# Moving five small steps of a hybrid-mixer kernel from GpSimd to VectorE

## The reference, cut to what matters

```python
for l in range(DEPTH):                                  # DEPTH = 2
    x = x + 0.5 * g1 * swiglu(modulate(rms_norm(x)), w1, w3, w2)
    x = x + g2 * hybrid_mixer(modulate(rms_norm(x)))
    x = x + 0.5 * g3 * swiglu(modulate(rms_norm(x)), w1, w3, w2)

def hybrid_mixer(h):
    q, k, v, qi, ki, wi, u = split(h @ w_in)
    q, k, qi, ki = rope(q), rope(k), rope(qi), rope(ki)  # partial rotary
    attn = dsa_attention(q, k, v, qi, ki, wi)   # indexer scores, top 128 keys per query, softmax
    y = gelu(s5_ssm(u))                         # state-space scan
    y = y * sigmoid(y @ glu_w + glu_b)
    return concat(rms_norm(attn), rms_norm(y)) @ w_out
```

## Time and profile before

| | us |
|---|---|
| median of 3 executions | 2107.84 |
| lowest, highest | 2107.36, 2109.96 |
| the profiled execution | 2107.84 |
| its span, first to last instruction | 2106.0 |
| PE busy | 2033.2 (97%) |
| DVE busy | 1317.8 (63%) |
| ACT busy | 694.5 (33%) |
| POOL busy | 261.0 (12%) |

### The profile page before, as it was taken

The page is one execution under the profiler, slowest core; times in us unless marked ns, Lnnn a source line. Parts: engine busy times, 40 slices in busy tenths (PEclk is TensorE's granted clock), DMA queues, the critical chain, the costliest instruction groups (busy, mean ns, idle before and its releaser), DMA issues.

```text
span 2106.0 us, 25359 instructions
## 1 busy us (share of the span) xinstructions
PE 2033.2 (97%) x9588; PEld 1639.6 (78%) x9588; DVE 1317.8 (63%) x2052; ACT 694.5 (33%) x1061; POOL 261.0 (12%) x231
## 2 busy tenths in 40 slices
PE   6999899999799999999999999999998999999998
PEld 5788778877577788888888877788775778888886
DVE  6778846566875654543466697375779656545334
ACT  4332222341444422222343322233334534213223
POOL 0006900400100000000000195040001000000000
PEclk8999999999799999999999999999997999999999
DMA  8465556342102354533337455544420125453332
GB/s 290 122 212 186 157 156 184 89 113 81 56 21 59 102 180 140 178 93 100 91 118 224 139 171 155 162 145 109 105 69 21 41 86 175 120 189 116 106 93 78
DMA packets 395985, 264.77 MB, mean 126 GB/s; under 512 B 56560, under 2 KB 371672, under 8 KB 395864
## 3 DMA queue, kind: packets, MB, share of 16 engines
q1 hardware_dynamic: 387360, 260.94, 40.9%
q10 hardware_dynamic: 8504, 2.22, 0.6%
HBM read 254.98 MB, written 6.29 MB: 124 GB/s over the span
## 4 chain that ended last, share of the span: by engine, by line
PE 63%; issue 22%; DVE 9%; ACT 4%; DMA 1%; ACTq 0%; SPq 0%; POOL 0%; DVEq 0%; POOLq 0%
PE ps L1700 18%; PE ps L1701 17%; PE ps L1702 17%; DVE w_lo L1002 2%; DVE mod_acc L1023 2%; PE ps L1980 2%; ACT w_hi L697 1%; PE ps L1999 1%; PE ps L1924 1%; PE ps L2007 1%; PE ps L1990 1%; PE ps L2072 1%; DVE x L1108 1%; DMA stage<-in_ffn_w 1%; PE ps L2077 1%
## 5 line engine op out<-in xcount | busy, mean ns | idle before, releaser
L1700 PE MATMUL ps<-h_hi,w_hi 128*128 128x512 f32 x1728 | 686.3, 397 | 15.6 <-DVE w_lo L1002 12.9
L1701 PE MATMUL ps<-h_lo,w_hi 128*128 128x512 f32 x1728 | 677.6, 392 | 0.0
L1702 PE MATMUL ps<-h_hi,w_lo 128*128 128x512 f32 x1728 | 677.2, 392 | 0.0
L1002 DVE TENSOR_TENSOR w_lo<-stage,w_hi 128x1024 fp32r<-128x1024 f32 (+2 forms) x322 | 394.3, 1247 | 117.3 <-ACT w_hi L697 113.5
L1700 PEld LDWEIGHTS ps<-h_hi,w_hi 128*128 128x128 f32 x1728 | 326.7, 189 | 95.9 <-issue 14.6
L1702 PEld LDWEIGHTS ps<-h_hi,w_lo 128*128 128x128 f32 x1728 | 327.1, 189 | 69.8
L1701 PEld LDWEIGHTS ps<-h_lo,w_hi 128*128 128x128 f32 x1728 | 327.2, 189 | 65.6 <-issue 0.5
L697 ACT ACTIVATE w_hi<-stage 128x1024 fp32r<-128x1024 f32 (+2 forms) x322 | 318.9, 1016 | 173.4 <-PE ps L1702 165.1
L1700 PE MATMUL ps<-g_hi,w_hi 128*128 128x512 f32 x704 | 276.7, 393 | 0.8 <-DVE g_lo L1317 0.8
L1701 PE MATMUL ps<-g_lo,w_hi 128*128 128x512 f32 x704 | 274.2, 389 | 0.0
L1702 PE MATMUL ps<-g_hi,w_lo 128*128 128x512 f32 x704 | 274.2, 389 | 0.0
(11 more groups left out here) (302 smaller groups left out, 1839.8 us busy)
## 6 DMA issues: line engine op xcount, KB each, us to landing
stage<-in_ffn_w SPq DMA_DIRECT2D x210, 512.0 KB, 4.4
mod_stage<-in_mod_w SPq DMA_DIRECT2D x144, 512.0 KB, 5.6
stage<-in_ffn_w SPq DMA_DIRECT2D x64, 448.0 KB, 4.0
stage<-in_w_in SPq DMA_DIRECT2D x20, 512.0 KB, 3.7
mod_first<-in_mod_w SPq DMA_DIRECT2D x16, 512.0 KB, 9.4
stage<-in_w_out SPq DMA_DIRECT2D x16, 512.0 KB, 4.2
x_in<-in_x SPq DMA_DIRECT2D x4, 512.0 KB, 5.8
stage<-in_w_in SPq DMA_DIRECT2D x8, 256.0 KB, 3.7
```

The source lines that it names most:

```text
L1002: V.tensor_tensor(w_lo[:, c % RING, 0:n], stage[:, c % RING, 0:n], w_hi[:, c % RING, 0:n].bitcast(F32), ALU.subtract).then_inc(w_split_lo. ...
L1700: mm(out, hi, rhs_hi, start=first, stop=False)
L1701: mm(out, hi, rhs_lo, start=False, stop=False)
L1702: return mm(out, lo, rhs_hi, start=False, stop=last)
```

## The change

The table `S5_LO_AT` is new: in steps e = 1, 2 and 3 DVE makes the low parts of the four gelu(y) tiles, in the new function `s5_lo`, which stands ahead of the weight split of the same step. At e = 4 DVE runs the whole of `rope(7)`, with scratch in `ssm_t` in place of `tmp_b`, where it ran one product before. GpSimd's `y_low` and `last_rope` are gone, with the two semaphores that tied the two engines in the last rotary.

```diff
+S5_LO_AT = {1: (0,), 2: (1, 2), 3: (3,)}
-DVE_STEPS, POOL_STEPS = 273, 86
+DVE_STEPS, POOL_STEPS = 275, 86
...
-        last_sin = Signal(sem("last_sin"), 1)
-        last_cos = Signal(sem("last_cos"), 1)
...
-                    part = tmp_b
+                    part = tmp_b if r < 7 else ssm_t
...
+                def s5_lo(m):
+                    dve.wait_ge(*y_hi.at(l, m))
+                    V.tensor_tensor(h_lo[:, AT + m, :], u_t[:, m].rearrange("p a b -> p (a b)"), h_hi[:, AT + m, :].bitcast(F32), ALU.subtract).then_inc(y_done.sem, 1)
...
+                    for m in S5_LO_AT.get(e, ()):
+                        s5_lo(m)
                     if e == LAST_ROPE:
-                        dve.wait_ge(*swap_mm.at(l, 7))
-                        V.tensor_tensor(ssm_t[:, 1, :], ps[:, ROPE_BANKS[7][1], :], rope_s[:], ALU.mult).then_inc(last_sin.sem, 1)
+                        rope(7)
...
-            def y_low(l, m):
-
-                pool.wait_ge(*y_hi.at(l, m))
-                Q.tensor_tensor(h_lo[:, AT + m, :], u_t[:, m].rearrange("p a b -> p (a b)"), h_hi[:, AT + m, :].bitcast(F32), ALU.subtract).then_inc(y_done.sem, 1)
-
-            def last_rope(l):
-
-                pool.wait_ge(*z_copy.at(l, ROPE_TILE[7]))
-                Q.tensor_tensor(ssm_t[:, 0, :], z_t[:, ROPE_TILE[7] % 2, :], rope_c[:], ALU.mult).then_inc(last_cos.sem, 1)
-                pool.wait_ge(*last_cos.at(l, 0))
-                pool.wait_ge(*last_sin.at(l, 0))
-                Q.tensor_tensor(q_t[:, AT - 1, :], ssm_t[:, 0, :], ssm_t[:, 1, :], ALU.add).then_inc(rope_done.sem, 1)
...
-                for m in range(ST):
-                    y_low(l, m)
-                last_rope(l)
```

## The result

The changed kernel took 2122.72 us in the median of four runs (2121.63 to 2124.24), the kernel before 2108.9 beside it (four runs, 2107.36 to 2110.13): ratio 1.0066, 95% interval [1.0049, 1.0084]. That is 13.8 us slower, where 5.6 were forecast, and above the range. A later series of the same changed kernel gave 2117.33 (2115.45 to 2119.85, five runs) against 2107.73 (21 runs): 1.0043 [1.003, 1.0055], +9.6 us. So "slower" was right, and the size was not.

The account below looks back on a forecast made before the run. VectorE was taken to set the pace through attention's first ten steps, TensorE afterwards. Terms 0.20 + 0.81 + 0.60 + 1.58 - 0.37 = +2.82 us a layer, doubled, gave 2113.5 us (+0.27%); 8-in-10 range 2109.5 to 2118.

Parts of the forecast that it names:

- the hand-over: End of attention's first ten steps: TensorE's values product waits 0.73 us for VectorE's first scaling, then TensorE sets the pace.
- The direct sum: VectorE's added work in attention steps 1 to 4, less recovered waits: +2.82 us a layer, +5.64 in all.
- idle 0.40 filled: Attention step 1: a 0.60 low part fills VectorE's 0.40 us idle before the weight split, net +0.20 a layer.
- split at 0.69: Attention step 2: without GpSimd the weight split is no longer stretched to 1.07; two low parts cost net +0.81.
- no wait at step 6: Attention step 6: VectorE's mask no longer waits for TensorE's logits, held up by GpSimd's rotary sum: -0.37 us a layer.
- Rival 1: Before the hand-over, added work lies beside waits and only recovered waits show: 2.3 us faster, 2105.5; chance 0.06.
- rival 4: Behind the hand-over, slack on TensorE swallows the shift: 2107.8 us; chance 0.04.
- The port, for and against: Attention: VectorE and GpSimd exclude each other at SBUF, so moving work might gain near zero; credited for 0.39 us a layer only.
- Nothing behind them waited for GpSimd, so that is worth nothing in itself: Attention's first stretch: removing GpSimd's 8.4 us of work there has no value of its own.
- The clock after the hand-over: Start of `glu`, both layers: TensorE's low clock may end sooner or later, -3.5 to +3.5 us at most for both.
- rival 3: Gap before the second FFN: TensorE's clock falls in both layers, 4.6 us more, 2118.1; chance 0.13.
- rivals 2: Gap before the second FFN: TensorE's clock stays up in both layers, 4.6 us less, 2108.9; chance 0.11.

Follow-up runs that it names:

- the repeat: The changed kernel, unaltered, run again beside the kernel before: 2117.33 us (five runs), ratio 1.0043.
- The rotary alone: Kernel before with the last rotary moved to VectorE, low parts left on GpSimd, and eight unused matmuls ahead of each second FFN: 2107.52 us, ratio 0.9995.
- the short delay: Kernel before with unused products of 1024 and 64 columns on VectorE at step 4 of attention, GpSimd's work kept: 2111.88 us over ten runs.
- the filled kernel before: Kernel before with eight unused matmuls in TensorE's 2.4 us gap ahead of each layer's second FFN: 2103.79 us, ratio 0.9979.
- the gap covered: Changed kernel with eight unused matmuls in TensorE's 2.4 us gap ahead of each layer's second FFN: 2112.56 us, ratio 1.0021 to the kernel before.
- a plain delay: Kernel before with three unused products (1024, 1024, 128 columns) on VectorE at step 4 of attention, GpSimd's work kept: 2117.86 us, ratio 1.0041.

## Why the prediction was right in part, and where it failed

- **What bounds the kernel: right.** VectorE's time before the hand-over came through to TensorE one for one in both layers, and TensorE's wait for the scaling stayed 0.73.
- **The direct sum: right.** 2.82 forecast, 2.79 and 2.78 measured (2.77 and 2.82 in the repeat), each step seen: idle 0.40 filled, split at 0.69, rotary 2.19, no wait at step 6. Rival 1 is out, and rival 4 too: no slack swallowed it. The rotary alone gave 1.18 for 1.21. The split of the low parts holds only for the whole change: alone they cost 1.0 and 0.8 more.
- **The port, for and against.** Weight splits of one shape took 0.69, or 1.07 beside GpSimd; a product 0.68 or 1.48; a pair 3.26 or 4.17. The Trainium skill's "SBUF — State Buffer", "Who interferes with whom", is borne out: who comes first goes first, and the other is stretched. The Trainium skill's "Perfetto Trace Analysis", "Optimizing Scalar/DVE Operations" (that moving work between the two may not help) is right in its outcome here, but not by the port: leaving the work on GpSimd would have cost VectorE 0.39 us a layer, and taking it cost 3.58 and gave only 0.39 and 0.37 back.
- **"Nothing behind them waited for GpSimd, so that is worth nothing in itself": wrong in size.** The shift of GpSimd's order in layer 1's first FFN costs 0.2 (repeat) to 1.1. I had looked at who waits for GpSimd, not at who shares a port with it.
- **The clock after the hand-over: mis-sized.** I gave its rise -3.5 to +3.5 about a middle of nothing. It came to +1.0 (repeat +0.7), and to +4.6 with the short delay. In the slowest run of the half with the rotary alone it was +4.9 (124.74 and 124.71 from hand-over to second FFN, against 122.18 and 122.41 in the filled kernel before). So even the bound of 3.5 was too small: the low clock after `glu` began lasted up to 9 us, over twice what before had, where I had allowed about double.
- **The step that failed: TensorE's clock, put at nothing in the forecast.** "What the sum does not hold is TensorE's clock": I left both second FFNs as in the one profile of before and gave that 0.66, and 0.13 to rival 3, "it falls in both layers". In both profiles of the changed kernel it falls in both layers: layer 1's start takes 11.19 and 11.03 in place of 6.43, +4.76 and +4.60, and with the gap covered it takes 6.44. The 6.43 of the one profiled execution was a single draw: before itself ran from 2103.3 to 2111.2 at granted clocks of 0.979 to 0.974. Nor were rivals 2 and 3 alike: in layer 0 the clock fell in all five profiles without the fill, so both layers staying up was the less likely. What brings the fall in layer 1 on, the shift or the missing work of GpSimd, stays open. That the repeat's median (2117.33) is within 1 us of rival 3's 2118.1 is partly luck: the run whose profile shows both falls took 2119.85.
- **What no rival had**: a low stretch at a third place, layer 1's projections (+1.68). It is in the first profile and not in the second. With it, the later rise (+1.0) and the port (+1.1), rival 3's 2118.1 becomes 2122, the time of the first series. Nor did I look at the stretch ahead of attention, where the profiles of the two filled kernels differ by 3.3 us at different granted clocks.

Shown by an edit: that covering the gap removes 4.6 us at each fall, and that a plain delay can bring a loss of 9.5, 5.9 of it its own length. Argued from profiles alone: the split of the first 13.8. Open: 3.2 of the 8.8 between the filled kernels, whether GpSimd's missing work has a part in the fall of layer 1, and what places a fall in one series and not in another.

## What to carry to other kernels

Work out the direct cost from the engine that paces the stretch; for the whole change that held here within 0.05 us a layer, for one of its halves alone it was 1.0 off. Then list each place where TensorE idles a few microseconds, price a clock fall at every one of them from rows at both levels, and take the one profiled execution as a draw, not as the default. Where such a gap ends in a wait that can't go, unused matmuls in it are worth more (here 4.6 us a layer where it falls) than the direct cost of the change under study (2.8); but at the low clock such matmuls are long and can become the pace themselves.

## What was not expected of the hardware

- One kernel has two times: the short delay gave 2108 to 2110 in five runs and 2114 to 2117 in the other five, at mean granted clocks of 0.977 and 0.974. The kernel before spread over 2103.3 to 2111.2 as well (0.979 to 0.974).
- The same eight matmuls of one column took 1.05 at the high level, and 1.69, 1.75 and 1.87 over executions in which the clock had fallen.
- GpSimd 0.3 us earlier reversed who is stretched at the shared port 700 us behind the edit, and the VectorE pair went from 3.26 to 4.17.
